# Decay rows kept on chip, selection masks in two steps and an earlier softmax scale in a two-layer encoder kernel

## What is computed

```
P = rmsnorm(x) @ w_in            # all projections
A: indexer scores -> top-k keys per query (k = 256, requests 132) -> attention over them
B: softmax(q k / 8 + F[t] - F[s]), s <= t, F = cumsum(log sigmoid(..)), 4 heads
C: attention to the own chunk and 8 chunks back, with a bias by distance
M: cross-attention to 256 memory tokens
x = x + concat(branch * silu(gate)) @ w_out
```

## Time and profile before

| | |
|---|---|
| runs shown, median (lowest to highest) | 1774.67 us (1774.35 to 1779.53) |
| the profiled execution, its own time | 1776.22 us |
| its span, first to last instruction | 1774.4 us |
| TensorE busy, share | 1724.7 us, 97% |
| VectorE busy, share | 1008.3 us, 57% |
| ScalarE, GpSimd busy | 692.6 us, 222.0 us |
| mean granted TensorE clock | 0.994 |

### The profile page before, as it was taken

One profiled execution on the slowest core, in us unless ns is written; L12 is line 12 of the kernel. 1 busy time (PEld: TensorE's weight loads), 2 busy tenths in 40 slices (PEclk: granted clock), 3 DMA queues, 4 the chain that ended last, 5 costly groups with the idle time before them and its releaser, 6 DMA issues.

```text
span 1774.4 us, 25988 instructions
## 1 busy us (share of the span) xinstructions
PE 1724.7 (97%) x8678; PEld 902.0 (51%) x8678; DVE 1008.3 (57%) x2709; ACT 692.6 (39%) x1657; POOL 222.0 (13%) x398
## 2 busy tenths in 40 slices
PE   7999999999999899999999999989999999999998
PEld 3544555555555455555444345545555544555553
DVE  3646876787778633332235288767877776333322
ACT  3542333433343344453224323333334433445531
POOL 0232211100000000001012332111000000000000
PEclk9999999999999999999999999999999999999999
DMA  6433533323122222112431425433231223220121
GB/s 249 116 138 90 180 133 132 140 77 105 45 111 90 91 67 76 58 53 64 120 121 49 162 79 178 133 140 121 78 108 42 107 93 96 71 97 36 43 73 46
DMA packets 57026, 177.75 MB, mean 100 GB/s; under 512 B 10128, under 2 KB 24304, under 8 KB 53824
## 3 DMA queue, kind: packets, MB, share of 16 engines
q1 hardware_dynamic: 39424, 125.88, 20.9%
q0 software_dynamic: 17472, 50.22, 8.6%
HBM read 149.09 MB, written 30.07 MB: 101 GB/s over the span
## 4 chain that ended last, share of the span: by engine, by line
PE 87%; DVE 6%; DMA 3%; ACT 2%; issue 2%; ACTq 0%; DVEq 0%; POOL 0%; SPq 0%
PE psX L828 58%; PE psT L786 9%; PE psS L944 6%; PE psX L1011 6%; DMA bias<-scratch_fp 2%; PE psS L856 2%; DVE lower L1221 1%; DVE work L1439 1%; PE psX L986 1%; PE psS L786 1%; PE psS L917 1%; PE psX L786 1%; DVE sc L1382 1%; PE psS L910 0%; PE psS L875 0%
## 5 line engine op out<-in xcount | busy, mean ns | idle before, releaser
L828 PE MATMUL psX<-wring,hT 128*128 128x512 f32 (+1 forms) x2592 | 1170.5, 593 | 5.4 <-ACT gate L1109 3.7
L828 PEld LDWEIGHTS psX<-wring,hT 128*128 128x128 f32 x2592 | 468.8, 191 | 480.5 <-issue 478.3
L1221 DVE TENSOR_SCALAR_CACHE_REDUCE lower<-sc,thr 128x640 uint8<-128x640 f32 (+5 forms) x462 | 407.3, 934 | 19.0 <-issue 12.7
L1160 ACT ACTIVATE work<-work,stat 128x256 f32<-128x256 f32 (+7 forms) x288 | 199.9, 694 | 309.5 <-DVEq L1442 306.4
L1169 ACT COPY work<-psT 128x512 f32<-128x512 f32 (+2 forms) x352 | 157.3, 489 | 339.2 <-PE psT L786 337.3
L786 PE MATMUL psT<-con,work 128*128 128x128 f32 x1080 | 158.9, 279 | 8.8 <-ACT kv L1128 8.8
L786 PEld LDWEIGHTS psT<-con,work 128*128 128x128 f32 x1080 | 123.1, 141 | 85.0 <-issue 73.2
L1439 DVE CUSTOM_DVE_ANT_0 work<-psS,bias 128x640 f32<-128x640 f32 (+7 forms) x144 | 103.8, 721 | 102.0 <-PE psT L786 36.5
L1439 DVE CUSTOM_DVE_ANT_0 work<-psS,sc 128x384 f32<-128x384 f32 (+5 forms) x48 | 42.8, 892 | 78.5 <-PE psT L786 74.8
L1487 POOL DMA_DIRECT2D scratch_oscr<-gate x54 | 30.3, 561 | 373.7 <-DVEq L1473 353.9
L944 PE MATMUL psS<-kv,qT 64*128 64x512 f32 (+3 forms) x384 | 69.9, 482 | 0.0
(11 more groups left out here) (195 smaller groups left out, 1537.7 us busy)
## 6 DMA issues: line engine op xcount, KB each, us to landing
wring<-in_w SPq DMA_DIRECT2D x20, 2048.0 KB, 8.4
cache<-in_kB SPq DMA_DIRECT2D x16, 512.0 KB, 8.0
cache<-in_vB SPq DMA_DIRECT2D x16, 512.0 KB, 5.2
cache<-in_kC SPq DMA_DIRECT2D x16, 512.0 KB, 6.5
cache<-in_vC SPq DMA_DIRECT2D x16, 512.0 KB, 4.9
scratch_oscr<-gate POOLq DMA_DIRECT2D x54, 128.0 KB, 2.0
hT<-scratch_oscr SPq DMA_DIRECT2D x18, 384.0 KB, 3.6
bias<-scratch_fp POOLq DMA_DIRECT2D x6, 1024.0 KB, 5.3
```

The costliest lines, as they stand in the source:

```text
L828: mm = pe.matmul(X.ap(use)[:, 0:w], lhs, wv[:, kt, 0:w], start=(kt == 0), stop=(kt == KT - 1))
L1160: nc.scalar.activation(x, x, ACT.Exp, scale=-1.0, bias=stats(p)[:, 0, i:i + 1], accum_out=stats(p)[:, 1, i:i + 1]).then_inc(probs.sem, 1)
L1221: v.tensor_scalar(lower[:, at:at + STRIP_L[t]], sc[:, o], thr[:, n:n + 1], 0.0, ALU.is_lt, ALU.add, accum_out=below[:, n:n + 1])
```

## The change

1. `rows_b` with its load per pack is replaced by `dec`, two arrays of two heads by 1024 keys, one in the bias region, one in `xr`. They are loaded once per layer in two parts, near (keys 0 to 255) and far (256 to 1023), by two DMAs each. For each query tile `close` (GpSimd) copies the tile's own 128 columns of two heads into `plain` and writes them back with the triangle added; after the logits `reopen` copies them back from `plain`, and `close` follows for the next tile and the same heads.
2. The step `wrow` (the running sums, the stores of the rows and the first loads) stands behind the gathering of the last requests' index queries (Q 3) and ahead of the first part of the ninth tile's projection B2 (Pp, B2); it stood behind the end of that projection (P, B2).
3. Each mask step becomes two, `ranks` and `mask`, and the pace is reckoned to (M1, 5) instead of (A2, 8).
4. The softmax scale becomes a step Z of its own, behind S of the next pack and ahead of that pack's L.

```diff
--- before.py
+++ after.py
@@ -120,7 +120,7 @@
 
 
     out = [(kind, i) for i in range(32) for kind in ("bit", "rest")]
-    return out + [("bit", 32)] + [("mask", t) for t in [ST_] + SEL_TILES]
+    return out + [("bit", 32)] + [(kind, t) for t in [ST_] + SEL_TILES for kind in ("ranks", "mask")]
 
 
 def program_order():
@@ -141,7 +141,7 @@
 
     count = lambda part: sum(STRIP_L[t] / 960 + 0.25 for t in part)
     cost = lambda x: {"bit": 0.5 + count(FIRST) * (x[1] < 32), "rest": count(REST)}.get(
-        x[0], 5.5 * STRIP_L.get(x[1], 0) / 960 + 1.0)
+        x[0], (3.3 if x[0] == "ranks" else 2.2) * STRIP_L.get(x[1], 0) / 960 + 0.5)
 
     def select(time):
         spare[0] += time
@@ -166,14 +166,13 @@
                 emit("T", prev, 0)
             turn_units()
         if pack:
-            if pack[0] == "A":
-                strip = ST_ if is_sample(pack) else pack[1]
-                while ("mask", strip) in rounds:
-                    emit("K", rounds.pop(0))
+            assert pack[0] != "A" or not rounds
             emit("S", pack)
             if is_sample(pack) and pack[2] + 1 < PAIRS:
                 j = pack[2] + 1
                 emit("Q", (pack[0], f"s{j}", j, 1))
+        if prev:
+            emit("Z", prev)
         if prev and not fresh:
             emit("T", prev, 0)
         if pack:
@@ -283,13 +282,13 @@
         emit("iw", 0)
         emit("P", "B1", ST_)
         emit("Q", 3)
+        emit("wrow")
         emit("Pp", "B2", ST_, 0, 3)
         emit("is", 2)
         emit("Pp", "B2", ST_, 3, 6)
         emit("is", 3)
         emit("TR", "B1", ST_)
         emit("P", "B2", ST_)
-        emit("wrow")
         emit("Q", ("B", "s0", 0, 1))
 
         units = [(c, t) for pair in (("B1", "B2"), ("C1", "C2")) for t in [ST_] + TILES[:NT] for c in pair][2:]
@@ -303,7 +302,7 @@
 
                 rounds += topk_steps()
                 spare[0] = 0.0
-                pace[0] = sum(cost(x) for x in rounds) / (units.index(("A2", ST_)) - units.index(("B1", 0)) - 1)
+                pace[0] = sum(cost(x) for x in rounds) / (units.index(("M1", 5)) - units.index(("B1", 0)) - 1)
             settle()
             if t < NT and c in ("B2", "C2", "M1", "A2"):
                 queue += packs_of(c[0], t)
@@ -513,7 +512,10 @@
         bias = sb("bias", H * 5 * P + SKEYS)
         gateA = bias[:, 0:(NT + 1) * W].rearrange("p (t c) -> p t c", c=W)
         gmem = bias[:, 0:D]
-        rows_b = bias[:, 0:2 * D]
+
+
+        dec = [bias[:, 0:2 * SEQ].rearrange("p (h c) -> p h c", h=2), xr[:, :, :]]
+        plain = bias[:, 2 * SEQ:2 * SEQ + H * P].rearrange("p (g h c) -> p g h c", g=2, h=2)
         strips = bias[:, 0:H * 5 * P].rearrange("p (h c) -> p h c", h=H)
         sbias_ = bias[:, H * 5 * P:]
 
@@ -623,7 +625,7 @@
         cache_loaded = [Signal(sem(f"cache{k}_loaded"), cache_loads[k::RING], lambda u: 16 * cdmas(u)) for k in range(RING)]
 
         b_packs = [p for p in packs if p[1][0] == "B" and not is_sample(p[1])]
-        pbias = Signal(sem("prompt_bias_loaded"), b_packs, lambda e: 16)
+        pbias = {e: Signal(sem(f"decays_{e}_loaded"), each(e), lambda e: 32) for e in ("near", "far")}
         masked = Signal(sem("prompt_bias_masked"), b_packs)
         strips_loaded = Signal(sem("strips_loaded"), each("C"), lambda e: 16)
         sbias_loads = [("B", j) for j in range(PAIRS)] + [("C", 0)]
@@ -675,11 +677,6 @@
             if br == "A":
                 return hT[:, first:first + n, t * P:(t + 1) * P]
             return gate[:, t, first * P:(first + n) * P].rearrange("p (g c) -> p g c", g=n)
-
-        def decays(pack):
-
-            n, L = heads(pack), blocks(pack) * P
-            return rows_b[:, 0:n * L].rearrange("p (h c) -> p h c", h=n)
 
         def tile_of(l, n):
 
@@ -1376,14 +1373,17 @@
                     t = s[1][1]
                     n, L = STRIPS.index(t), STRIP_L[t]
                     a, eq, lo = sc[:, SC_OFF[t]:SC_OFF[t] + L], equal[:, 0:L], lower[:, 0:L]
-                    count_below([t])
-                    v.tensor_scalar(eq, a, thr[:, n:n + 1], -BIG, ALU.is_equal, ALU.mult)
-                    dve.drain()
-                    v.tensor_tensor_scan(a, eq, eq, 0.0, ALU.add, ALU.bypass)
-                    v.tensor_scalar(share[:, 0:1], below[:, n:n + 1], -BIG, BIG * (L - STRIP_K[t]), ALU.mult, ALU.add)
-                    dve.drain()
-                    v.tensor_tensor(share[:, 1:2], share[:, 0:1], a[:, L - 1:L], ALU.add)
-                    dve.drain()
+                    if s[1][0] == "ranks":
+
+                        count_below([t])
+                        v.tensor_scalar(eq, a, thr[:, n:n + 1], -BIG, ALU.is_equal, ALU.mult)
+                        dve.drain()
+                        v.tensor_tensor_scan(a, eq, eq, 0.0, ALU.add, ALU.bypass)
+                        v.tensor_scalar(share[:, 0:1], below[:, n:n + 1], -BIG, BIG * (L - STRIP_K[t]), ALU.mult, ALU.add)
+                        dve.drain()
+                        v.tensor_tensor(share[:, 1:2], share[:, 0:1], a[:, L - 1:L], ALU.add)
+                        dve.drain()
+                        continue
                     v.scalar_tensor_tensor(out=a, in0=a, scalar=share[:, 1:2], in1=eq, op0=ALU.is_lt, op1=ALU.mult)
                     dve.drain()
                     v.scalar_tensor_tensor(out=a, in0=lo, scalar=-BIG, in1=a, op0=ALU.mult, op1=ALU.add)
@@ -1416,7 +1416,7 @@
                             b_ = sbias_[:, 0:L]
                         elif br == "B":
                             dve.wait_ge(*masked.on(p))
-                            b_ = decays(p)[:, i, :]
+                            b_ = dec[h // 2][:, h % 2, 0:L]
                         elif br == "C":
                             if (h, t) == (0, 0):
 
@@ -1440,7 +1440,7 @@
                         if i >= heads(p) - 2:
                             last.then_inc(S.empty(u).sem, 1)
                         dve.drain().then_inc(logits.sem, 1)
-                elif k == "T" and s[2] == buffers(s[1])[-1]:
+                elif k == "Z":
 
                     p = s[1]
                     br, t, h0, nh = p
@@ -1504,19 +1504,33 @@
                         pool.dma_start(d["xr"][h * P:(h + 1) * P, :], d["xl"][h:h + 1, :].to_broadcast([P, XL])
                                        ).then_inc(lines.sem, 16)
 
-            def prompt_bias(p):
+            def decays(part):
+
+                c0, c1 = {"near": (0, 2 * P), "far": (2 * P, SEQ)}[part]
+                for g_ in range(2):
+                    src = bass.AP(d["fp"].tensor, 2 * g_ * SEQ + c0, [[0, P], [SEQ, 2], [1, c1 - c0]])
+                    pool.dma_start(dec[g_][:, :, c0:c1], src).then_inc(pbias[part].sem, 16)
+
+            def close(p):
 
                 _, t, h0, n = p
-                L = (t + 1) * P
-                src = bass.AP(d["fp"].tensor, h0 * SEQ, [[0, P], [SEQ, n], [1, L]])
-                pool.dma_start(decays(p), src).then_inc(pbias.sem, 16)
-
-            def prompt_mask(p):
-
-                own = decays(p)[:, :, blocks(p) * P - P:]
-                pool.wait_ge(*pbias.on(p))
-                g.tensor_tensor(own, own, con[:, C_TRI:C_TRI + P].unsqueeze(1).to_broadcast([P, heads(p), P]), ALU.add
-                                ).then_inc(masked.sem, 1)
+                part = "near" if t < 2 else "far"
+                pool.wait_ge(*pbias[part].on(part))
+                tri = con[:, C_TRI:C_TRI + P].unsqueeze(1).to_broadcast([P, 2, P])
+                for g_ in range(h0 // 2, (h0 + n) // 2):
+                    g.tensor_copy(plain[:, g_], dec[g_][:, :, t * P:(t + 1) * P])
+                pool.drain()
+                for g_ in range(h0 // 2, (h0 + n) // 2):
+                    last = g.tensor_tensor(dec[g_][:, :, t * P:(t + 1) * P], plain[:, g_], tri, ALU.add)
+                last.then_inc(masked.sem, 1)
+                pool.drain()
+
+            def reopen(p):
+
+                _, t, h0, n = p
+                for g_ in range(h0 // 2, (h0 + n) // 2):
+                    g.tensor_copy(dec[g_][:, :, t * P:(t + 1) * P], plain[:, g_])
+                pool.drain()
 
             def own_halves(q, j, hp, heads_, gg=0):
 
@@ -1605,9 +1619,10 @@
                     store(d["fp"], work[0:4, 3, :], f_dma.sem)
                     store(d["fs"], work[0:32, 2, P:P + SKEYS], f_dma.sem)
                     pool.wait_ge(*f_dma.on("out"))
-                    prompt_bias(packs_of("B", 0)[0])
+                    decays("near")
                     sample_bias("B", 0)
-                    prompt_mask(packs_of("B", 0)[0])
+                    decays("far")
+                    close(packs_of("B", 0)[0])
                 elif k == "Q" and s[1] in range(PAIRS):
 
                     j = s[1]
@@ -1647,11 +1662,12 @@
                         sample_bias(*sbias_loads[h0 + 1])
                     elif br == "B":
                         pool.wait_ge(*logits.on(last_logits))
-                        i = b_packs.index((l, p))
```

(10 more changed lines are left out.)

## The result

The changed kernel takes 1749.48 us (median of 4 runs, 1748.32 to 1750.13) against 1775.18 for the kernel before (4 runs, 1774.35 to 1779.53; the 1774.67 of the table ahead of the prediction is the median of the first three): a ratio of 0.985, 95% interval 0.9833 to 0.9867. The profiled execution took 1748.32 with a span of 1746.5, 27.9 less than the span before. The forecast was 1750, in a range of 1744 to 1764.

What follows compares the result with a forecast made beforehand. TensorE bounds the kernel, busy 1724.7 of 1774.4 us; only its idle time and low-clock loss can go. 14.0 + 10.1 + 2.5 - 2.0 = 24.6 us off a median of 1774.7 gives 1750, range 1744 to 1764.

Steps and rivals of the forecast that it cites:

- Sum 14.0 us: B, both layers: decay rows on chip remove TensorE's gap and the low clock behind it, 6.7 and 7.3 us.
- 0 us: Ahead of the first B logits: earlier running sums remove a wait of about a us that cost TensorE nothing.
- Gone are 2.62 + 1.7: M, layer 1: the earlier softmax scale removes V's 2.62 us gap and 1.7 us lost to the low clock.
- 2.5 - 2.0 us: Split mask steps gain 2.5 us in M; the faster selection pace costs 2.0 us, both layers together.
- The tail, 5.1 us: M, behind V's gap: further TensorE waits, 2.5 us per layer, of which half was to go.
- The pace was to cost 2.0: B and C: more selection per unit, one tight pair in C, 1 us lost per layer.
- 33 us per layer: GpSimd's compute on closings and reopenings, at 0.72 us per copy or addition; it was 11 us per layer.
- (a): Rival: the new pace takes back the M gain, VectorE leads in C's tight pair; 1763 us, chance 0.21.
- (b): Rival: the load was not what counted or VectorE is late in B anyway; 0 to 5 us, 1772, chance 0.09.
- (c): Rival: GpSimd's added compute in B blocks VectorE, making the kernel slower; 1792 us, chance 0.06.
- (d): Rival: masks not done before A or loads still awaited; no chance of its own, counted in (b).
- VectorE's share: Sign that the forecast is right: VectorE's busy share in B and C rises by 4 to 6%.

Runs made afterwards that it cites:

- Parts 3 and 4 alone: Kernel before with split mask steps, faster selection pace and earlier softmax scale, decay loads and running sums as before: 1750.54 us, ratio 0.9852.
- parts 2 to 4: Changed kernel with the decay rows loaded per pack again, everything else as changed: 1750.53 us, ratio 0.9856.
- part 2 undone: Changed kernel with the running sums put back behind the ninth tile's B2 projection: 1768.89 us, ratio 0.996.
- second order of the loads: Changed kernel with running sums late again and both the far decay loads and sample bias loads issued behind the first closing: 1765.56 us, ratio 0.9933.
- the last kernel: Changed kernel with the selection pace weighted by the length of the units: 1745.22 us, ratio 0.9821.

## Why the prediction was right, and where it was wrong

**The total** was right, 1749.5 for 1750, and the places named were those where the time came from: B's gap, V's gap in M, the low clock behind both. That it was right by these four terms is in part luck: three of them were credited wrongly. Parts 3 and 4 alone give the same time (1750.54), and without the step that was put at 0 the change gives 7 us (1768.89, beside 1776.28 for the kernel before).

**Part 1: the step that failed is "Sum 14.0 us"** as what part 1 gives. The time was there to gain, and it was gained. But that step took the 9.26 us wait for the load as the load's own cost. The same view had shown C1's weights issued by SP 0.52 us behind it, and loads of this queue at tile 5 awaited some 4 us; I did not ask why this one took twice as long. It was a collision, decided by a few tenths of a us. With parts 3 and 4 the two issues lie 0.8 to 0.9 us apart instead of 0.5, and then the gap is gone with the loads still made (1750.54). What part 1 gives beside the other three is 1.05 us of the median, within the error. That it makes the time steadier isn't shown: with it the runs lie within 1.8 us, with parts 2 to 4 within 6.3, but with parts 3 and 4, all loads still made, within 0.6.

**Part 2: the step that failed is "0 us".** I counted that GpSimd "waits for no DMA after the first tile" and looked no further at the first tile. The changed kernel issues six loads there, and then a drain sits between copies and addition. The earlier sums hide it; without them the change loses 19.4 us, three quarters of what it gives. Of these the far loads at the drain are 8.4 (1768.89 to 1760.52); the rest is not taken apart. Parts 1 and 2 are one edit: together worth a us here, part 1 without part 2 is a loss against parts 3 and 4 alone of some 18 (1768.89 to 1750.54).

**Part 4: the step that failed is "Gone are 2.62 + 1.7"** for M, and the same in layer 2, 8.3 of its 10.1 us. Alone the part gives 21.1, undone in the full change 4.9. The V gaps were read rightly as waits for the scale, and L was said to be put off by the scale's length only; but L itself waits behind the undivided mask step, and with it the exp, ScalarE's gate copy and TensorE. Alone, the part takes M's waits from 9.97 to 8.09 us in both layers and the low clock, together 5.3 for the 8.3. Some 11 of its 21.1 us lie in B: waits from 11.63 to 4.33 and 3.5 from the clock, the early V gaps and, by its shift, most of the collision. The shortfall in the full change is what part 3 has taken already. A single number for a part exists only beside a statement of which others are there.

**Part 3**, 2.5 - 2.0 us, was sized too small where it stands alone (7.0), since it halves all of M's waits and not its tail only. The tail, 5.1 us, was to be halved; it went to 1.36 + 1.28 = 2.6, a gain of 2.4 for 2.5. The pace was to cost 2.0; the four new waits at C's head make 0.62 + 0.21 + 0.43 + 0.70 = 1.96. They stand in the two pairs behind the one that the prediction named: VectorE runs four selection steps from 359.88 us on, with only short attention work between them, the last beyond the end of the tight pair, and comes to a gate at 377.37. Net 0.5, and undoing the part costs 1.3.

**GpSimd's compute:** 33 us per layer were forecast, 23.6 measured, since the copy was priced at the addition's 0.72 and takes 0.40. Even the lower bound of 0.60, from an operation of half the size, was too high. The groups of the changed kernel (ns: min/median/max):

```profile
L1521 POOL COPY bias<-bias x16: 391/403/404, 149.4 to 1159.1; 128x256 f32<-128x256 f32 x16
...
L1524 POOL TENSOR_TENSOR bias<-bias,con x16: 724/727/734, 156.9 to 1159.6; 128x256 f32<-128x256 f32 x16
```

**The rivals.** (a) did not come about: the M part stayed gained. The sign that it named, TensorE idle ahead of a psT or psX operation behind B, is there at a small scale only, 0.62 and 0.21 us. (b) got 9% and was nearer to the mechanism than the forecast in its first half, that taking the loads away was not what counted: the gap goes with the loads still made. But VectorE was not late there either, and the time, 1772, is far off, because the gap does go. (c) fell: no counting operation over 1281 ns, and the gate's scale is now at most 427 where it was 901. (d) did not come about: the masks are done before A, and GpSimd issues 8 decay loads in place of 24.

**The margin of 3.3 us** between the 24.6 forecast and the 27.9 of the spans: 1.76 is waits in layer 1's A stage, 0.82 two waits in B, and 0.19 the second early V gap, which is 1.09 and not 0.90; 0.5 has no place. The A stage has a part in the change: the step Z stands ahead of L there as well. All five traces of kernels without part 4 have these waits, 1.75 to 1.77 us, and none of the nine with it, so they are part 4's too.

**Signs.** TensorE has no wait over 1 us in B and the clock stays at 1.00, as forecast. VectorE's share was to rise by 4 to 6%; in the windows above it rose by 10 points in B and 3 in C. What was to be added came out: over the same 967 records of TensorE (175.0 to 344.2 us before, 174.1 to 336.2 now) VectorE is busy 122.9 and 133.6 us, 10.7 more for the three steps of 10.6. By the prediction's own chances, with half of (b) as no change, faster would be 0.895 and not 0.87.

## What to carry to other kernels

Where one load out of a series takes twice as long as its neighbours, look at what else was issued within a us of it: here it was a collision, and an edit elsewhere that shifts one issue by a few tenths of a us can make or mend it. Before crediting a part with a gain, run it undone in the full change and alone in the old kernel; if the two differ, the parts overlap or need each other. Filler work that is handed out by the unit should follow the units' lengths, or the short ones become the chain, here for one or two us per layer.

## What the runs showed of the hardware that was not expected

- A drain on GpSimd between two of its operations kept it idle for 6.76 and 8.08 us (changed kernel, layers 1 and 2), 7.23 and 7.87 (part 2 undone), 6.64 and 5.53 (second order of the loads), where its own loads had been issued some 3 to 5 us before and were still under way, and for 0.15 to 0.55 us in the steady state. In layer 2 of the last kernel it was 11.18. Where the far loads stand ahead of the drain, the next operation starts 2.0 to 2.1 us behind the landing of the last of them, in ten cases of ten. Taking two loads from ahead of it brought 7.23 to 3.84; with none under way by the semaphores it was still 3.68, in both layers, and that is not explained.
- A load of 896 KB is awaited 4.1 us alone, and 7.6 to 10.2 us if it is issued between 0.4 us behind and 0.6 us ahead of a 2 MB load. From 0.8 to 1.0 us ahead it is 3.9 to 4.2 in four cases and 6.1 and 6.9 in two.
- GpSimd's copy of 128x256 in fp32 takes 0.40 us and its addition of two inputs 0.73. VectorE's operation on seven columns took 0.39 us instead of 0.17 in 12 of its 64 records in the changed kernel, where it had never been over 0.17 before. The longest, from 1122.75 us, started 0.02 us behind one of the copies of `reopen` and ended with it. The Trainium skill (SBUF — State Buffer, Who interferes with whom) says that an operation of VectorE with two SBUF inputs contends with one of GpSimd's that reads SBUF; this one has two, and the trace agrees. It cost nothing that can be seen.
